# Token norm taken out of the expert stage's input: a raw stream for queries, scores and dot products, and two query units split by token tile

## The chip, the cores and the metric

The kernel runs on 1 core of one Trainium2 chip. The metric is the device time of one execution in microseconds, the median of several. The engines of the core are PE (matmuls, with its weight loads shown apart as PEld), DVE, ACT, POOL and SP; the last two and others issue DMAs.

## The reference

256 tokens of width 1024, float32. A first block (mixing layer, then a product-key expert layer), then a second block of two layers with feed-forward parts. The change touches only the entry of the expert layer:

```python
hn = rmsnorm(h, norm2_g)                       # h * rsqrt(mean(h^2) + eps) * g, per token
qp = (hn @ wq).reshape(128, 8, 2, 128)         # per tile of 128 tokens: 8 heads, 2 halves
s  = einsum('thcd,hcnd->thcn', qp, subkeys)    # 128 scores a half
v1, i1 = top_k(s[:, :, 0], 16); v2, i2 = top_k(s[:, :, 1], 16)
sc, p  = top_k(all 256 sums v1 + v2, 16)       # 16 experts a head, of 16384
gates  = softmax(sc)
act    = gelu(einsum('td,thkd->thk', hn, u[eidx]))
h      = h + einsum('thk,thkd->td', gates * act, v[eidx])
```

## The kernel before

One program with an instruction list per engine; the order of the work is written out by hand and the engines meet at semaphores. The stream is kept as `hT`, features on partitions, 8 blocks of 128 features (`KT`) by 256 tokens; the two tiles of 128 tokens are `own(0)` and `own(1)`. Weights come as "units" of 1 MB through a ring of 4 slots, loaded by SP: 14 for the input projection, 4 for the output projection, 8 query units (`peerq`, one head each), then those of the second block. A unit's weights may be loaded when the unit four before is done (`unit_done`).

Around the change, in order of time:

- Output projection, four units. For each, DVE adds the result to `hT` (L1168, `h_new`) and ACT squares it (L540, `norm_sq`). DVE fills its gaps with `ada_ops`, weighted sums for the second block's modulation.
- Norm: PE sums the squares with a ones matrix (`sums`, L1629), ACT makes Ln and Exp (`rsqrt`, L545 and L547, `norm_rs`), DVE writes `xn = h * norm2 * rstd` in 16 pieces, token tile 0 first (L1172).
- Queries: unit 0 is taken by token tile (`query_first`, L1889); its scores for tile 0 (`scores(0)`, L1865) come between the tiles. Units 1 to 7 run over all 256 tokens (`features`, L1666), with scores of other heads between them. ACT copies queries (L574, L659, L664) and scores (L654) out of PSUM. `BATCH` lists nine batches of scores: batches 0 and 1 are heads 0 and 1 of tile 0, each later one has two heads.
- Behind units 0 to 3 PE transposes `xn` into token rows in PSUM (`row_transposes`, L1852, `hn_t` counts four); DVE multiplies gathered rows with them.
- Selection on DVE (`top_rows`, `top_pairs`, `top_index`, L1180 to L1248) makes indices, `idx_ready`. DVE does batches 0 and 1, waits for `hn_t` 4, and then takes the 256 rows of the u table (128 experts a token, for 2 tiles) one by one (`u_row`, L1271), with the next batch's selection at rows 6, 9, 12 and 15 of every 32.
- POOL issues the gathers (L496), one for each expert slot, 128 rows of 4 KB. `SEQ` is their order: 38 u gathers, then u and v in turn. `GRING` = 16 slots hold them; from the 17th gather on, POOL waits, for each pair, for the uses of the pair 16 before (`u_used`, `v_used`). It waits for the indices of batch 2 at gather 32 (counted from 0).
- PE, after the last scores, sums the ada products column by column (`columns`, L1877, one-column matmuls), and then accumulates the v rows with a diagonal of weights as the stationary operand (`v_row`, L1928). The weights are gate times Gelu of the dot product; ACT makes Gelu (L690) and the diagonals (L698). The last two of the nine batches of scores are in PSUM banks that the v sums of tile 1 take later.
- The first load of subkeys and iota is issued by POOL when all of `hT` is new (L478 to L480, `peer_in`).

Of the kernel before, what the change touches and what calls it, by code (L numbers as in the profile page):

```python
# [19 lines left out]
ALU = mybir.AluOpType  # L20
# [4 lines left out]
D = 1024  # L25
T = 256
KT = D // P
# [71 lines left out]
def build(nc, xT, cols_d, w_d, alibi_d, masks_d, ident_d, tri_d, blk_d, sbmask_d, iota_d, subk_d, rg_d,  # L99
          u_d, v_d, out):  # L100
    with ExitStack() as ctx:
# [267 lines left out]

        gg, gf2 = small[:, 48:56], small[:, 56:64]  # L370
# [77 lines left out]
        def _(pool):  # L448
# [29 lines left out]
            pool.wait_ge(h_new, H_MIX)  # L478
# [48 lines left out]
        def _(act):  # L527
# [120 lines left out]
            rsqrt(1)  # L648

            def scores_in(b):  # L650

                tt, h, n = BATCH[b]
                act.wait_ge(sc_ps, b + 1)
                a.activation(flat(S[f"s{tt}"][:, 2 * h:2 * h + 2 * n, :]), bank[4 + b % 2][:, 0:256 * n], ACT.Copy  # L654
                             ).then_inc(sc_in, 1)
            for j in range(8):
                if j == 0:
                    act.wait_ge(sc_first, 1)
                    a.activation(S["qpT"][:, 0:2, own(0)], bank[5][:, 0:256].rearrange("p (b t) -> p b t", b=2), ACT.Copy  # L659
                                 ).then_inc(q0_in, 1)  # L660
                    scores_in(0)
                    g = UNIT0["peerq"]
                    act.wait_ge(unit_done, g + 1)
                    a.activation(S["qpT"][:, 0:2, own(1)], bank[g % 2][:, 0:256].rearrange("p (b t) -> p b t", b=2),  # L664
                                 ACT.Copy).then_inc(unit_out[g % 2], 1)
                    continue
                read_unit(UNIT0["peerq"] + j, ACT.Copy, flat(S["qpT"][:, 2 * j:2 * j + 2, :]))
                if j == 1:
                    scores_in(1)
                elif j % 2:  # L670
                    scores_in(2 + j // 2 - 1)
# [15 lines left out]
            def gelu(gp):  # L687
# [3 lines left out]
                             S["act"][:, gp // 4, 32 * (gp % 4):32 * (gp % 4) + 32], ACT.Gelu).then_inc(act_gelu, 1)  # L691
# [236 lines left out]
        def _(dve):  # L928
# [427 lines left out]
            dve.wait_ge(hn_t, 4)  # L1356
            for n in range(ROWS):
                u_row(n)
# [264 lines left out]
        def _(pe):  # L1623
# [11 lines left out]

            def unit_start(g, it=0, regs=False):
# [205 lines left out]
            sums(1, range(0, 4))  # L1842
# [379 lines left out]
```

## Time and profile before

| | us |
|---|---|
| median of 3 runs | 1664.23 |
| lowest, highest | 1662.99, 1664.76 |
| the profiled execution's own time | 1667.39 |
| its span, first to last instruction | 1665.6 |

| engine | busy us | share | instructions |
|---|---|---|---|
| PE | 1408.3 | 85% | 7372 |
| PEld | 1036.3 | 62% | 7372 |
| DVE | 1026.2 | 62% | 1832 |
| ACT | 492.8 | 30% | 827 |
| POOL | 588.1 | 35% | 630 |

The profile shows one execution. A busy share is an average over stages with different limits, so each stage is read by itself. "Idle before" an instruction is followed by what released it, as the profile infers it; "issue" means that the engine waited for nothing that the profile shows. A matmul in float32 appears as two records, each with its weight load; ends of matmuls are modelled and overlap the next start.

### The profile page before, as it was taken

The page shows a single profiled execution, that of the slowest core. Times are in us where ns is not written, and L with a number is a line of the kernel's source. Part 1 is how long each engine was busy: PE and PEld are TensorE (multiplying, and loading weights), DVE is VectorE, ACT ScalarE, POOL GpSimd, SP SyncE. Part 2 cuts the span into 40 slices and gives each one's busy share as a digit, 9 for nine tenths or more (in the row PEclk, how much of TensorE's full clock was granted, in tenths as well). Part 3 has the DMA queues.
Part 4 walks back from the last instruction along what each step waited for, and adds up shares of the span by engine and source line. Part 5 has one row for each costly group of instructions (what it writes and reads, how often), then busy time and mean ns, then how long its engine had stood idle before and what let it go on. Part 6 is the DMA issues. An engine that isn't in the chain of part 4 may idle for free.

```text
span 1665.6 us, 20006 instructions
## 1 busy us (share of the span) xinstructions
PE 1408.3 (85%) x7372; PEld 1036.3 (62%) x7372; DVE 1026.2 (62%) x1832; ACT 492.8 (30%) x827; POOL 588.1 (35%) x630
## 2 busy tenths in 40 slices
PE   6889989677777777787777789889999998989998
PEld 5778878322222222332222259889999996789998
DVE  4796669856547464674644455778787447554544
ACT  2222202111111211121121126344444556444342
POOL 1320045566666666666666620012221002100000
PEclk9999998799999998799999999999999998999999
DMA  9655687999999999999899974659885441135450
GB/s 371 254 204 185 252 349 267 366 371 340 380 377 350 353 363 360 365 370 373 336 353 365 371 309 160 245 216 317 315 318 196 139 152 76 68 139 178 184 189 25
DMA packets 113930, 454.10 MB, mean 273 GB/s; under 512 B 12032, under 2 KB 29584, under 8 KB 100544
## 3 DMA queue, kind: packets, MB, share of 16 engines
q0 software_dynamic: 81616, 297.84, 47.4%
q1 hardware_dynamic: 32240, 155.31, 25.6%
q8 instruction: 41, 0.67, 0.2%
q14 instruction: 33, 0.27, 0.0%
HBM read 452.06 MB, written 1.05 MB: 272 GB/s over the span
## 4 chain that ended last, share of the span: by engine, by line
PE 55%; POOL 12%; issue 11%; DMA 10%; DVE 8%; ACT 2%; another core or an unknown queue 1%; SPq 0%; POOLq 0%; DVEq 0%; ACTq 0%
PE psum L2020 14%; POOL arena L496 12%; PE psum L2034 7%; PE psum L1683 7%; PE psum L1928 7%; DMA arena<-v_d,arena 6%; PE psum L1666 6%; DMA arena<-u_d,arena 2%; PE psum L1653 2%; PE psum L1696 1%; PE psum L1877 1%; DVE arena L1271 1%; DVE wlo L955 1%; PE psum L1650 1%
## 5 line engine op out<-in xcount | busy, mean ns | idle before, releaser
L1928 PE MATMUL psum<-arena 128*128 128x512 f32 x952 | 493.4, 651 | 173.2 <-DMA arena<-v_d,arena 125.0
L1928 PEld LDWEIGHTS psum<-arena 128*128 128x128 f32 x952 | 175.0, 201 | 489.4 <-DMA arena<-v_d,arena 277.6
L1271 DVE CUSTOM_DVE_ANT_0 arena<-arena,psum 128x1024 f32<-128x1024 f32 x256 | 305.1, 1219 | 212.7 <-DMA arena<-u_d,arena 167.1
L496 POOL DMA_INDIRECT arena<-u_d,arena x256 | 244.3, 954 | 201.1 <-issue 74.1
L496 POOL DMA_INDIRECT arena<-v_d,arena x256 | 243.3, 950 | 86.4 <-issue 73.2
L955 DVE TENSOR_TENSOR wlo<-ring,whi 128x2048 fp32r<-128x2048 f32 x74 | 169.5, 2291 | 107.8 <-ACT whi L564 107.8
L698 ACT ACTIVATE arena<-ident,arena 128x128 f32<-128x128 f32 x238 | 84.4, 394 | 431.2 <-PE psum L1928 191.1
L2020 PE MATMUL psum<-xh,whi 128*128 128x256 f32 x704 | 201.1, 286 | 9.4 <-DVE xl L949 5.6
L2020 PE MATMUL psum<-xl,whi 128*128 128x256 f32 x704 | 200.5, 285 | 0.0
L2020 PE MATMUL psum<-xh,wlo 128*128 128x256 f32 x704 | 200.4, 285 | 0.0
L564 ACT ACTIVATE whi<-ring 128x2048 fp32r<-128x2048 f32 x74 | 140.7, 1901 | 27.8 <-PE psum L1683 23.4
L2020 PEld LDWEIGHTS psum<-xh,whi 128*128 128x128 f32 x704 | 136.5, 194 | 10.7 <-issue 6.3
L2020 PEld LDWEIGHTS psum<-xl,whi 128*128 128x128 f32 x704 | 136.5, 194 | 0.0
L2020 PEld LDWEIGHTS psum<-xh,wlo 128*128 128x128 f32 x704 | 136.5, 194 | 0.0
L511 POOL DMA_DIRECT2D second<-w_ada x64 | 46.3, 724 | 194.2 <-DVE second L983 113.6
L2034 PE MATMUL psum<-fh,dhi 128*128 128x256 f32 x352 | 100.7, 286 | 0.0
L2034 PE MATMUL psum<-fl,dhi 128*128 128x256 f32 x352 | 100.5, 286 | 0.0
L2034 PE MATMUL psum<-fh,dlo 128*128 128x256 f32 x352 | 100.5, 285 | 0.0
L961 DVE TENSOR_TENSOR dlo<-ring,dhi 128x1024 fp32r<-128x1024 f32 x44 | 53.9, 1225 | 69.0 <-ACT dhi L570 69.0
L570 ACT ACTIVATE dhi<-ring 128x1024 fp32r<-128x1024 f32 x44 | 46.5, 1057 | 137.3 <-PE psum L2034 137.3
L1683 PE MATMUL psum<-xh,whi 128*128 128x256 f32 x288 | 85.0, 295 | 1.8 <-DVE xl L949 1.5
L1683 PE MATMUL psum<-xh,wlo 128*128 128x256 f32 x288 | 82.1, 285 | 0.0
(287 smaller groups left out, 2272.2 us busy)
## 6 DMA issues: line engine op xcount, KB each, us to landing
ring<-w_ffn SPq DMA_DIRECT2D x44, 1536.0 KB, 6.6
second<-w_ada POOLq DMA_DIRECT2D x64, 384.0 KB, 6.5
arena<-w_ada SPq DMA_DIRECT2D x50, 384.0 KB, 7.3
ring<-w_inproj SPq DMA_DIRECT2D x14, 1024.0 KB, 7.9
ring<-w_qkv SPq DMA_DIRECT2D x12, 1024.0 KB, 5.1
ring<-w_l0in SPq DMA_DIRECT2D x10, 1024.0 KB, 4.9
ring<-w_peerq SPq DMA_DIRECT2D x8, 1024.0 KB, 7.7
sq<-w_ada SPq DMA_DIRECT2D x14, 384.0 KB, 6.6
```

The source lines that it names most:

```text
L496: g.indirect_dma_start(S["rows"][:, p % GRING, :], None, u_d if kind == "u" else v_d, bass.IndirectOffsetOnAxis(S["idx"][:, n // SLOTS, n ...
L564: a.activation(r32(S[f"whi{g % 2}"]), slot(g, 0, 2048), ACT.Copy).then_inc(w_hi, 1)
L570: a.activation(r32(S[f"dhi{j % 2}"]), slot(g, 2048, 3072), ACT.Copy).then_inc(d_hi, 1)
L698: a.activation(S["diag"][:, c % DIAGS, :], ident[:, :], ACT.Copy, scale=S["wts"][:, n // SLOTS, n % SLOTS:n % SLOTS + 1]).then_inc(diag_re ...
L955: v.tensor_tensor(r32(S[f"wlo{g % 2}"]), slot(g, 0, 2048), S[f"whi{g % 2}"], ALU.subtract).then_inc(w_lo, 1)
L961: v.tensor_tensor(r32(S[f"dlo{j % 2}"]), slot(g, 2048, 3072), S[f"dhi{j % 2}"], ALU.subtract).then_inc(d_lo, 1)
L1271: v.tensor_tensor_reduce(row, row, xrow[n // SLOTS], 1.0, 0.0, ALU.mult, ALU.add, S["act"][:, n // SLOTS, n % SLOTS:n % SLOTS + 1]).then_i ...
L1666: ins = t.matmul(bank[g % 2][:, b * T:(b + 1) * T], w[:, b, k, :], src[:, k, :], start=(k == 0), stop=(k == KT - 1))
L1683: ins = t.matmul(bank[g % 2][:, b * T:(b + 1) * T], r32(w[i][:, b, k, :]), r32((hi, lo)[j][:, k, :]), start=(b == 0 and k == 0 and i + j = ...
L1928: ins = t.matmul(vacc[tt][:, at], S["diag"][:, c % DIAGS, :], row[:, at], start=(n % SLOTS == 0), stop=(n == LAST_PE[tt]))
L2020: ins = t.matmul(bank[g % 2][:, b * T:(b + 1) * T], r32(w[i][:, b, k, :]), r32((xh, xl)[jj][:, k, :]), start=(b == 0 and k == 0 and i + jj ...
L2034: ins = t.matmul(bank[2 + n // 2][:, 256 * (n % 2):256 * (n % 2) + 256], r32(w[i][:, n, :]), r32(S[f"{('fh', 'fl')[jj]}{u % 2}"]), start=( ...
```

## The change

The token factor of the norm, 1/rms, is the same for all features of a token, so it can be applied behind a matmul. `xn` becomes `h * norm2`, without the factor, written per unit right after each residual add (two instructions of 128x256 instead of four of 128x128). The factor is computed per token on partitions (`token_sums`, one-column matmuls with the squares as stationary operand; `token_rstd` on ACT, 128x2) and applied where the scores leave PSUM (`scores_in`, scale operand) and inside Gelu. The first half of the token sums stands before the last output unit, the second half behind the first query tile.

Query units 0 and 1 are both taken by token tile, tile 0 first: PE's order is query(0, tile 0), second half of the token sums, scores(0), query(1, tile 0), query(0, tile 1), scores(1), two groups of transposes, query(1, tile 1), then units 2 to 7 as before. The transposes of tile 0 thus stand ahead of unit 2, and those of tile 1 behind units 2 and 3. DVE waits for `hn_t` 2 before the first u row and for 4 before row 128. POOL loads subkeys and iota after the recurrent part's transposes (`rec_t` 2).

```diff
@@ POOL
-            pool.wait_ge(h_new, H_MIX)
+            pool.wait_ge(rec_t, 2)
             g.dma_start(S["subk"], subk_d).then_inc(peer_in, 16)
@@ ACT
-            rsqrt(1)
+            def query_in(j, tt):
+                g = UNIT0["peerq"] + j
+                src, dst = (bank[5], bank[1])[j] if tt == 0 else bank[g % 2], S["qpT"][:, 2 * j:2 * j + 2, own(tt)]
+                if tt == 0:
+                    act.wait_ge(sc_first, j + 1)
+                    done = q0_in
+                else:
+                    act.wait_ge(unit_done, g + 1)
+                    done = unit_out[g % 2]
+                a.activation(dst, src[:, 0:256].rearrange("p (b t) -> p b t", b=2), ACT.Copy).then_inc(done, 1)
+            def token_rstd():
+                act.wait_ge(norm_sum, 2)
+                seq.mark(a.activation(lnv[:, 0:2], NORM[:, 0:2], ACT.Ln, scale=1.0 / D, bias=col("eps")))
+                seq.wait()
+                a.activation(rs_tok, lnv[:, 0:2], ACT.Exp, scale=-0.5).then_inc(norm_rs, 1)
             def scores_in(b):
...
+                a.activation(flat(S[f"s{tt}"][:, 2 * h:2 * h + 2 * n, :]), bank[4 + b % 2][:, 0:256 * n], ACT.Copy,
+                             scale=rs_tok[:, tt:tt + 1]).then_inc(sc_in, 1)
+            query_in(0, 0)
+            token_rstd()
+            act.wait_ge(norm_rs, 2)
+            scores_in(0)
+            query_in(1, 0)
+            query_in(0, 1)
+            scores_in(1)
+            query_in(1, 1)
@@ gelu
-                             S["act"][:, gp // 4, 32 * (gp % 4):32 * (gp % 4) + 32], ACT.Gelu).then_inc(act_gelu, 1)
+                             S["act"][:, gp // 4, 32 * (gp % 4):32 * (gp % 4) + 32], ACT.Gelu,
+                             scale=rs_tok[:, gp // 4:gp // 4 + 1]).then_inc(act_gelu, 1)
@@ DVE
-            dve.wait_ge(norm_rs, 2)
-            for tt in range(TT):
-                for k in range(KT):
-                    v.scalar_tensor_tensor(xn[:, k, own(tt)], hT[:, k, own(tt)], col("norm2", k), rstd[:, own(tt)],
-                                           ALU.mult, ALU.mult).then_inc((xg_ready, norm_out)[tt], 1)
+                dve.wait_ge(h_new, j + 1)
+                for k in (2 * j, 2 * j + 1):
+                    v.tensor_scalar(xn[:, k, :], hT[:, k, :], col("norm2", k), None, ALU.mult).then_inc(norm_out, 1)
...
-            dve.wait_ge(hn_t, 4)
+            dve.wait_ge(hn_t, 2)
             for n in range(ROWS):
+                if n == SLOTS:
+                    dve.wait_ge(hn_t, 4)
@@ PE
+            def token_sums(ks):
+                for k in ks:
+                    pe.wait_ge(norm_sq, 8 + k + 1)
+                    for tt in range(TT):
+                        ins = t.matmul(NORM[:, tt:tt + 1], sq[:, k, own(tt)], ones[:, 0:1],
+                                       start=(k == 0 and tt == 0), stop=(k == KT - 1), skip_group_check=True)
...
-            sums(1, range(0, 4))
+            token_sums(range(0, 4))
...
-            sums(1, range(4, KT))
...
+            query(0, 0)
+            token_sums(range(4, KT))
+            scores(0)
+            query(1, 0)
+            query(0, 1)
+            scores(1)
+            row_transposes(0)
+            row_transposes(1)
+            query(1, 1)
+            for j in range(2, 8):
                 g = UNIT0["peerq"] + j
                 unit_start(g)
-                if j == 0:
...
+                features(g, xn)
                 if j < 4:
                     row_transposes(j)
-                if j == 1:
-                    scores(1)
-                elif j and j % 2:
+                if j % 2:
                     scores(2 + j // 2 - 1)
```

`query(j, tt)` is the old `query_first` for both units: for each feature block both column halves in turn, unit 0 tile 0 waiting for each block of `xn`.

## Rows read from the trace of the kernel before

**Rows 1.** The page's chart in 40 slices, the DMA row.
```profile
DMA  9655687999999999999899974659885441135450
```

**Rows 2.** All gathers of the v table by their source line: durations, first and last start.
```profile
L496 POOL DMA_INDIRECT arena<-v_d,arena x256: 932/937/1937, 285.1 to 971.8; - x128
```

**Rows 3.** Stretches: length, busy (count) PE, PEld, DVE, ACT, POOL, clock, DMA share, GB/s.
```profile
220.00:240.00 20.00, 15.10 (x64) 11.88 (x63) 7.78 (x27) 1.19 (x2) 11.22 (x12) 0.86 1.02 411
240.00:260.00 20.00, 19.31 (x93) 16.83 (x92) 19.72 (x60) 2.39 (x4) 10.42 (x12) 0.97 0.96 366
260.00:280.00 20.00, 19.31 (x121) 17.64 (x119) 19.52 (x47) 7.32 (x12) 7.69 (x8) 0.97 0.59 185
280.00:300.00 20.00, 10.69 (x52) 11.15 (x51) 19.90 (x39) 4.23 (x12) 14.99 (x16) 0.50 1.00 381
300.00:320.00 20.00, 12.95 (x34) 7.76 (x35) 14.10 (x53) 1.61 (x4) 7.49 (x8) 0.68 0.87 332
```

**Rows 4.** Timeline of DVE: start, us, line, operation, count, idle before and releaser.
```profile
195.53 0.69 DVE L1168 TENSOR_TENSOR hT<-psum,hT 128x512 f32<-128x512 f32 x1 [4.77 <-PE psum L1666]
198.84 4.29 DVE L1172 SCALAR_TENSOR_TENSOR xn<-hT,cols,rstd 128x128 f32<-128x128 f32 x16 [2.62 <-ACT rstd L547]
...
205.10 0.48 DVE L1180 MAX8 arena<-arena 128x8 f32<-128x128 f32 x2
...
217.32 0.49 DVE L1180 MAX8 arena<-arena 128x8 f32<-128x128 f32 x2 [2.63 <-ACT arena L654]
...
238.82 1.22 DVE L1271 CUSTOM_DVE_ANT_0 arena<-arena,psum 128x1024 f32<-128x1024 f32 x1 [11.70 <-PE psum L1852]
...
246.82 0.48 DVE L1180 MAX8 arena<-arena 128x8 f32<-128x128 f32 x2
...
273.07 0.18 DVE L1245 CAST arena<-arena 128x32 int32<-128x32 f32 x1
```

**Rows 5.** Timeline of PE matmuls, same columns.
```profile
199.34 4.02 PE L1889 MATMUL psum<-xn,ring 128*128 128x128 f32 x32 [1.49 <-DVE xn L1172]
203.84 0.71 PE L1865 MATMUL psum<-arena 128*128 128x128 f32 x4 [0.47 <-ACT arena L659]
204.38 3.74 PE L1889 MATMUL psum<-xn,ring 128*128 128x128 f32 x32
...
238.62 2.07 PE L1865 MATMUL psum<-arena 128*128 128x128 f32 x8
...
275.98 10.26 PE L1877 MATMUL psum<-ones,ring 128*128 128x1 f32 x60
...
309.88 24.15 PE L1928 MATMUL psum<-arena 128*128 128x512 f32 x52
```

**Rows 6.** Timeline of POOL's issues, same columns.
```profile
214.89 1.03 POOL L496 DMA_INDIRECT arena<-u_d,arena  x1 [17.24 <-DVE arena L1245]
...
241.97 0.94 POOL L496 DMA_INDIRECT arena<-u_d,arena  x1 [7.39 <-DVE arena L1271]
...
276.40 0.93 POOL L496 DMA_INDIRECT arena<-u_d,arena  x1 [5.67 <-DVE arena L1271]
...
302.49 0.94 POOL L496 DMA_INDIRECT arena<-v_d,arena  x1 [0.30 <-issue]
314.11 0.94 POOL L496 DMA_INDIRECT arena<-u_d,arena  x1 [10.68 <-PE psum L1928]
```

**Rows 7.** Timeline of PE weight loads around its two slow stretches.
```profile
223.94 5.70 PEld L1666 LDWEIGHTS psum<-xn,ring 128*128 128x128 f32 x27
231.96 0.19 PEld L1666 LDWEIGHTS psum<-xn,ring 128*128 128x128 f32 x1 [2.33 <-issue]
...
291.32 0.29 PEld L1877 LDWEIGHTS psum<-ones,arena 128*128 128x128 f32 x1 [1.33 <-issue]
...
307.51 2.42 PEld L1877 LDWEIGHTS psum<-ones,arena 128*128 128x128 f32 x11 [1.81 <-issue]
```

**Rows 8.** DVE groups by line, first 60 us: count, busy, mean.
```profile
L1009 DVE TENSOR_SCALAR arena<-hT,cols 128x256 f32<-128x256 f32 x8 | 2.2, 346 | 0.0
```

More of the change, by code:

```diff
@@ L367, in flat @@
             return ap.rearrange("p a b -> p (a b)")
+        rs_tok = small[:, 1:3]
         gg, gf2 = small[:, 48:56], small[:, 56:64]
@@ L653, in scores_in @@
                 act.wait_ge(sc_ps, b + 1)
-                a.activation(flat(S[f"s{tt}"][:, 2 * h:2 * h + 2 * n, :]), bank[4 + b % 2][:, 0:256 * n], ACT.Copy
-                             ).then_inc(sc_in, 1)
-            for j in range(8):
-                if j == 0:
[L658 to L666, printed above, removed]
+                a.activation(flat(S[f"s{tt}"][:, 2 * h:2 * h + 2 * n, :]), bank[4 + b % 2][:, 0:256 * n], ACT.Copy,
[9 more added lines that the diff above has]
+            for j in range(2, 8):
                 read_unit(UNIT0["peerq"] + j, ACT.Copy, flat(S["qpT"][:, 2 * j:2 * j + 2, :]))
-                if j == 1:
-                    scores_in(1)
-                elif j % 2:
+                if j % 2:
                     scores_in(2 + j // 2 - 1)
@@ L1857, in scores @@
                 tt, h, n = BATCH[b]
-                if b:
+                if b < 2:
+                    pe.wait_ge(q0_in, b + 1)
+                else:
                     wait_unit_out(pe, UNIT0["peerq"] + h + n - 1)
@@ L1878, in columns, with query @@
                     ins.then_inc(mcol_ps, 1)
-            def query_first(tt):
-                g = UNIT0["peerq"]
+            def query(j, tt):
+                g = UNIT0["peerq"] + j
                 w = slot(g, 0, 2048).rearrange("p (b k c) -> p b k c", b=2, k=KT)
-                at = (bank[5], bank[g % 2])[tt]
-                for b in range(2):
-                    for k in range(KT):
-                        if b == 0:
-                            pe.wait_ge((xg_ready, norm_out)[tt], (KT + 2, KT)[tt] + k + 1)
+                at = (bank[5], bank[1])[j] if tt == 0 else bank[g % 2]
+                if tt == 0:
+                    unit_start(g)
+                elif j == 1:
+                    pe.wait_ge(q0_in, 2)
+                for k in range(KT):
+                    if j == 0 and tt == 0:
+                        pe.wait_ge(norm_out, KT + k + 1)
+                    for b in range(2):
                         ins = t.matmul(at[:, b * P:(b + 1) * P], w[:, b, k, :], xn[:, k, own(tt)],
-                                       start=(k == 0), stop=(k == KT - 1))
+                                       start=(k == 0 and b == 0), stop=(k == KT - 1), skip_group_check=True)
                 ins.then_inc((sc_first, unit_done)[tt], 1)
-            for j in range(8):
+            query(0, 0)
[7 more added lines that the diff above has]
+            query(1, 1)
+            for j in range(2, 8):
                 g = UNIT0["peerq"] + j
                 unit_start(g)
-                if j == 0:
-                    query_first(0)
-                    pe.wait_ge(q0_in, 1)
-                    scores(0)
-                    query_first(1)
-                else:
-                    features(g, xn)
+                features(g, xn)
                 if j < 4:
                     row_transposes(j)
-                if j == 1:
-                    scores(1)
-                elif j and j % 2:
+                if j % 2:
                     scores(2 + j // 2 - 1)
```

4 lines of the change are left out of this document (added).

## The prediction

> **What bounds the kernel now.** I read the page's chart first. DMA stands at 9 tenths from the sixth slice to the twenty-third [rows 1]; a slice is 41.6 us. That is the expert stage: 512 gathers of 128 table rows (0.52 MB each), issued by POOL through a ring of 16 slots, the first at 214.89 us [rows 6], the last at 971.8 [rows 2]. So 757 us of the 1665.6 go by the transfers, one gather every 1.48 us, where POOL alone could issue one in 1.24 (22 issues from 276.40 to 302.49 [rows 6], 26.1/21). PE, DVE and ACT have room in this stage. The stage gets shorter in two ways only: it starts earlier, or the DMA idles less.
>
> Next I looked for that idle time in stretches [rows 3]. From 220 to 240 the share is 1.02, then 0.96, 0.59, 1.00, 0.87. Lost are 0.8 + 8.2 + 2.6 = 11.6 us. The 8.2 comes because POOL may not issue gather 32 before DVE has made the indices of batch 2 (273.07 [rows 4], gather at 276.40 [rows 6]); the 2.6 because the 55th gather needs the slot of the first v row, which PE uses at 309.88 [rows 5], and is let go at 314.11 after 10.68 us [rows 6]. I call that issue the gate. At the gate every slot but one is landed or used, before and after the change alike, so I carry the rest over whole: the end moves as the gate moves, unless the DMA has no idle left to lose.
>
> Why is DVE late? Its first dot product runs at 238.82 after 11.70 us of waiting for the fourth group of transposes [rows 4], which PE reaches only after four query units. And PE is slow there: 27 weight loads follow each other at 0.21 us until 229.6, the next ones are at 231.96 and on with up to 2.33 us of "issue" between, to 237.6 [rows 7]; the same from 290.0 to 307.2 in the column sums [rows 7]. Both begin 14 to 15 us after POOL began a run of issues without a pause (214.89, 276.40) and end 3 to 4 us after it stopped (234.58 and 303.43, from the idle in [rows 6]). The trace shows no cause beyond "issue". I take this as a pattern of two cases, not as a law; the answer hangs on it.
>
> **The change, part by part.**
> *Stream and norm.* Before: last residual 195.53, then sum of squares, Ln and Exp, DVE's 16 multiplies from 198.84 (4.29 us), the first query tile on PE at 199.34, top-16 at 205.10 [rows 4, 5]. Now xn is h times a column: 8 instructions at 0.27 (2.2/8 [rows 8]), six of them in gaps; the last two end at 196.2 + 0.6 = 196.8. Query tile 0 has six of eight k-steps ready when PE leaves the out projection at 195.5. Token sums replace column sums: 16 records per half. They are nowhere in the trace; nearest are the one-column matmuls of the ada sums, 0.22 each at half clock (11 in 2.42 [rows 7]), and for full clock the queries' 0.114 (3.65/32 [rows 5]). So 1.8 to 3.5 us a half; I take 1.8, since the clock stayed full at this place in the queries. First half: 1.8 against 1.9 for the old form, nothing. PE then: query(0,0) 195.7 to 199.4, sums to 201.2, scores(0) 0.5. From scores to top-16 took 205.10 - 203.84 = 1.26 [rows 4, 5]; here Ln and Exp (about 0.95, as from sums to 198.84 before) end at 202.2 and the copy follows, so top-16 starts at 202.8. Gain 2.3 (0.5 to 2.5). The scale operands in the copies and in Gelu cost nothing I can find; the subkey load (1 MB), now at 170 instead of 196.5, is moved past no other POOL work of use and meets an idle-enough DMA.
> *Two units by token tile.* PE: query(1,0), query(0,1), 3.65 each, scores(1) from 209.0: its scores are out at 210.2, before DVE is free at 212.4. Batch 1 starts then instead of at 217.32 [rows 4]: 4.9 us, of which 2.3 were already counted. DVE is through at 222.2.
> *hn_t 2 instead of 4.* Transposes 0 and 1 are done at 210.7. DVE starts its dot products at 222.2 instead of 238.82: 16.6 us. It then needs seven rows and scores(2). Before, that was at 246.82 [rows 4] and scores(2) were out at 240.7 [rows 5]; the wait had a cover of 6 us. Now row 6 lands near 231 (gathers at 1.28 us from 215, two query weights between them) and scores(2), unhindered, are out at 230.3 + 0.8. The cover is gone: whatever PE loses before scores(2) is lost to DVE and to batch 2.
> *PE to the gate.* From the end of scores(2) to the column sums are 35.3 us (240.7 to 276.0 [rows 5]), all weights loaded ahead. Then 48 columns in 96 records: 0.11 each for some 3 us, then 0.22, as the first 60 in 10.26 say [rows 5]; the granted clock there is 0.50 [rows 3]. Then the first v row, 4.2 us to the gate.
>
> **The forecast: both slow stretches come again, as long as before.** The first falls on PE at 227 (14.5 us after 212.6), in query unit 3, and adds 8.0: scores(2) at 238.3 instead of 240.7. DVE's batch 2 starts at 239.1 instead of 246.82, its indices are made at 265.5, gather 32 goes at 268.6. Columns start at 273.6; the second stretch begins at 282.2, after 27 + 25 records. POOL fills its ring by 268.6 + 27 = 295.9, the stretch ends at 300, some 8 records later; 36 are left, 8 us. First v row at 308, gate at 312: 2 us earlier. Of the 16.6 us only 2 arrive, since PE, not DVE, opens the gate. On the profiled execution: 1667.39 (span 1665.6) - 2 = 1665.4; on the median of the runs shown, 3.2 lower, **1662.2**. A gain or loss of 2 comes with the first stretch being 3 us longer or shorter: own range 1660 to 1666.
>
> **Rivals.**
> *No slow stretches on the path.* They could be tied to what PE happened to fetch there. Then scores(2) are out at 231, indices at 258, gather 32 at 262, column sums 265.7 to 284, v row done at 288, before POOL is through with the 54th issue (289). The DMA has work without a gap: 11.6 + 2.3, less 1 for the thin backlog at 262, is 13: 1651. If only the second stretch comes, v row at 300 and gate at 304: 10 us, 1654. For it: 240 to 258 shows PE dense beside gathers and no such stretch. Against it: both were there in the one trace.
> The Trainium skill, page "Runtime: NRT & Kernel Launch", section "Instruction fetch mechanics", says that engines fetch ahead in blocks and that crossing a block is mostly hidden. By that rule alone the slow stretches are no lasting property and this rival holds; the "issue" rows of the trace do not agree with it at these two places.
> *A short first stretch.* It begins a few us later, when scores(2) are nearly out, and hits the rest of the units: gate 6 earlier, 1658.
> *The first stretch gets longer (slower).* Before, it ended when POOL stopped at 234.58, because the ring was full and DVE had not begun. Now DVE frees slots, and POOL goes on until DVE is held at its seventh row: 22 gathers, to 239.6. If the stretch ends 3.5 us after that, PE at 1.6 to 2.4 us a record pair still has 12 pairs of its 21 to do at 243: scores(2) at 245.6, 5 us later than before. Batch 2 is where it was (246.4 against 246.82), gather 32 too, but the column sums start at 281, have 53 records done at 289.6, and end at 315: gate 5 later, 1669. It decides from the point where PE's last scores(2) matmul is later than 240.7. For it: both stretches ended with POOL's stop. Against it: two cases only, and PE may be past unit 3 when it begins.
>
> **How the numbers follow.** Forecast 0.38; no or only one stretch 0.27 (1650 to 1656); short first stretch 0.10; longer one 0.25. Less than 0.2% (3.3 us) can't be told from no change. Faster is below 1660.9: 0.27 + 0.10 + 0.06 of the forecast's low side = 0.43. Slower is above 1667.6: 0.25. Within: 0.32. Gains and losses hold both; the range leaves one in ten on either side: 1651 to 1669.5.
>
> **What will show it.** Top-16 at 202.8; batch 1 without idle before it; the first dot product near 222; then an idle of DVE before batch 2 (the forecast: 7 to 9 us, released by scores; none if no stretch comes; 14 if it is longer). Gather 32 near 269, gate near 312. Wrong would be the whole argument if the stretches from the gate on did not repeat, or if the DMA share after it changed.

## The result, and the profile after

The changed kernel takes 1673.71 us (median of 5 runs, 1671.32 to 1678.61) against 1664.76 of the kernel before beside it (5 runs): ratio 1.006, 95% interval 1.0043 to 1.0077. It is slower by about 9 us, clear of noise (the interval is 7 to 13 us); forecast were 1662.2 with a range up to 1669.5. The profiled execution has a span of 1676.8 us, 11.2 more than before. The last gather of the v table starts at 981.7 instead of 971.8 [rows 2], so nearly all of it is lost before that point.

DVE's timeline (columns as in [rows 4]):
```profile
196.95 0.61 DVE L1187 TENSOR_SCALAR xn<-hT,cols 128x256 f32<-128x256 f32 x2
...
202.66 0.49 DVE L1194 MAX8 arena<-arena 128x8 f32<-128x128 f32 x2 [3.05 <-ACT arena L673]
...
212.17 0.48 DVE L1194 MAX8 arena<-arena 128x8 f32<-128x128 f32 x2
...
221.94 1.21 DVE L1285 CUSTOM_DVE_ANT_0 arena<-arena,psum 128x1024 f32<-128x1024 f32 x1
...
247.20 0.49 DVE L1194 MAX8 arena<-arena 128x8 f32<-128x128 f32 x2 [17.18 <-ACT arena L673]
```
The first four rows are what the change was to do: top-16 2.4 us earlier than in [rows 4], batch 1 5.2 earlier, the first dot product 16.9 earlier. The fifth shows where it went: DVE waits 17.18 us for scores(2), and batch 2 starts at 247.20, where it was at 246.82.

POOL's issues, to be read against [rows 6]:
```profile
212.45 1.03 POOL L497 DMA_INDIRECT arena<-u_d,arena  x1 [40.79 <-DVE arena L1259]
...
238.66 0.94 POOL L497 DMA_INDIRECT arena<-u_d,arena  x1 [0.30 <-issue]
251.57 0.94 POOL L497 DMA_INDIRECT arena<-u_d,arena  x1 [11.98 <-DVE arena L1285]
...
276.79 0.94 POOL L497 DMA_INDIRECT arena<-u_d,arena  x1 [5.67 <-DVE arena L1285]
...
302.88 0.94 POOL L497 DMA_INDIRECT arena<-v_d,arena  x1 [0.31 <-issue]
324.63 0.93 POOL L497 DMA_INDIRECT arena<-u_d,arena  x1 [20.82 <-PE psum L1962]
```
The 22nd gather goes at 238.66 without a break, six more than the 16 of before; gather 32 is where it was; the gate, the 55th, is let go at 324.63 instead of 314.11, after 20.82 us instead of 10.68.

PE's timeline:
```profile
196.02 3.73 PE L1922 MATMUL psum<-xn,ring 128*128 128x128 f32 x32
199.59 1.84 PE L1657 MATMUL psum<-ones,sq 128*128 128x1 f32 x16
...
221.21 5.79 PE L1692 MATMUL psum<-xn,ring 128*128 128x256 f32 x26
...
228.04 0.38 PE L1692 MATMUL psum<-xn,ring 128*128 128x256 f32 x1 [1.04 <-issue]
...
243.45 0.59 PE L1879 MATMUL psum<-ident,xn 128*128 128x128 f32 x2 [1.02 <-issue]
244.36 2.08 PE L1894 MATMUL psum<-arena 128*128 128x128 f32 x8 [0.33 <-ACT arena L575]
...
277.83 5.16 PE L1894 MATMUL psum<-arena 128*128 128x128 f32 x40 [0.69 <-ACT arena L575]
285.92 6.42 PE L1906 MATMUL psum<-ones,ring 128*128 128x1 f32 x31 [2.94 <-ACT arena L673]
292.98 0.16 PE L1906 MATMUL psum<-ones,ring 128*128 128x1 f32 x1 [0.64 <-issue]
...
305.58 0.16 PE L1906 MATMUL psum<-ones,ring 128*128 128x1 f32 x1 [2.63 <-issue]
...
320.10 10.28 PE L1962 MATMUL psum<-arena 128*128 128x512 f32 x19
```
PE is slow from 226.6 to 243.5 (by its weight loads), 16.9 us where it was 8, and scores(2) are out at 246.4 instead of 240.7 [rows 5]: 5.7 lost. The columns begin at 285.92 instead of 275.98: another 4.2 lost between. From there to the v row it is 34.2 (33.9 before).

Of those 4.2, 0.9 are on PE itself: its next 64 records take 15.25 us, where they took 14.34, at a granted clock of 0.92 instead of 0.98. Another 0.2 are in the last scores (5.16 against 4.97), and the remaining 3.1 are on ACT. L574 and L575 are its copies of a query unit, L654 and L673 its copies of the scores. First two of its rows before, then four after:
```profile
231.98 0.60 ACT L574 ACTIVATE arena<-psum 128x512 f32<-128x512 f32 x1 [14.69 <-remote]
...
276.18 0.60 ACT L654 ACTIVATE arena<-psum 128x512 f32<-128x512 f32 x1 [0.41 <-PE psum L1865]
```
```profile
228.76 0.60 ACT L575 ACTIVATE arena<-psum 128x512 f32<-128x512 f32 x1 [14.31 <-remote]
...
281.02 0.69 ACT L673 ACTIVATE arena<-psum,small 128x512 f32<-128x512 f32 x1 [0.42 <-PE psum L1894]
285.18 0.69 ACT L673 ACTIVATE arena<-psum,small 128x512 f32<-128x512 f32 x1 [3.47 <-remote]
291.60 0.69 ACT L673 ACTIVATE arena<-psum,small 128x512 f32<-128x512 f32 x1 [5.73 <-remote]
```
ACT has slow stretches of its own, and its first one begins sooner than PE's. Query unit 2 is through on PE at 223.8 before and at 220.9 after; ACT copies it only at 231.98 and 228.76, some 8 us later. Nothing on the path waits for that copy. The second one does cost: the copy at 285.18 is the eighth, for which the columns wait (`sc_in` 8); the one at 291.60 is the ninth, for which they do not. Before, all nine copies were through by 276.8, just as gather 32 was issued (276.40). After, the copies are 6.7 us later and gather 32 is not, and the last two are caught. Whether ACT had such a stretch there before too can't be seen: from 280.0 on it had nothing to do until DVE's 32nd dot product was out (291.6).

The windows (columns as in [rows 3]) sum it up: DMA share 0.83 where it was 0.96, and 0.45 where it was 0.87. That is 2.6 and 8.4 us of transfers lost, 11.0 together; the span grew by 11.2.
```profile
220.00:240.00 20.00, 10.09 (x41) 7.42 (x40) 9.84 (x21) 0.60 (x1) 14.99 (x16) 0.79 1.02 412
240.00:260.00 20.00, 16.96 (x70) 14.33 (x70) 12.53 (x46) 1.88 (x3) 4.68 (x5) 0.78 0.83 320
...
300.00:320.00 20.00, 12.79 (x62) 13.16 (x61) 15.43 (x55) 0.20 (x1) 2.90 (x4) 0.50 0.45 180
```

### The profile page after: what moved, and what is told of

Same layout as the page of the kernel before. It is cut to its first block, busy times and chain, and to the rows that moved or that the text cites. A ratio compares the mean times of both kernels' runs of the same rounds, so it can differ in the third digit from the quotient of the medians.

```text
span 1676.8 us, 20097 instructions
## 1 busy us (share of the span) xinstructions
PE 1414.7 (84%) x7420; PEld 1044.8 (62%) x7420; DVE 1023.5 (61%) x1824; ACT 494.9 (30%) x828; POOL 586.7 (35%) x630
## 4 chain that ended last, share of the span: by engine, by line
PE 52%; POOL 14%; issue 12%; DMA 10%; DVE 7%; another core or an unknown queue 3%; ACT 2%; POOLq 0%; SPq 0%; DVEq 0%
PE psum L2054 14%; POOL arena L497 14%; PE psum L2068 7%; PE psum L1709 7%; DMA arena<-v_d,arena 7%; PE psum L1962 5%; PE psum L1692 4%; PE psum L1679 2%; PE psum L1906 2%; DMA arena<-u_d,arena 2%; PE psum L1722 1%; DVE arena L1285 1%; PE psum L1676 1%; PE psum L1824 1%
## 5 line engine op out<-in xcount | busy, mean ns | idle before, releaser
L2054 PE MATMUL psum<-xl,whi 128*128 128x256 f32 x704 | 200.5, 285 | 0.0
L2054 PE MATMUL psum<-xh,wlo 128*128 128x256 f32 x704 | 200.4, 285 | 0.0
L1709 PE MATMUL psum<-xl,whi 128*128 128x256 f32 x288 | 82.7, 287 | 0.0
```

Source lines behind the costliest of these rows:

```text
L1709: ins = t.matmul(bank[g % 2][:, b * T:(b + 1) * T], r32(w[i][:, b, k, :]), r32((hi, lo)[j][:, k, :]), start=(b == 0 and k == 0 and i + j = ...
L2054: ins = t.matmul(bank[g % 2][:, b * T:(b + 1) * T], r32(w[i][:, b, k, :]), r32((xh, xl)[jj][:, k, :]), start=(b == 0 and k == 0 and i + jj ...
```

## The experiments

They ran on six chips, and there are two kinds. On some the kernel before takes 1664 to 1668 us and the slow stretches are there; on the others it takes 1590, and none is seen in any trace. Each ratio is to the kernel before on the same chip. In the quoted expectations the letters of the theories hold for that text alone; from e12 on, A2 is that POOL's run of issues brings the stretch about, B2 that the busy DMA does.

**Holding the gathers back (e1, e7, e13, e15).** The edit, before POOL's 17th gather:
```diff
+                if p == GRING:
+                    pool.wait_ge(sc_in, 3)
```


> The changed kernel with one wait more: POOL issues gather 16 only when the scores of batch 2 are copied out (sc_in 3), so that its first run of issues ends after 16 gathers, as in the kernel before. Theory A (PE's slow stretch lasts until POOL stops issuing): POOL stops at about 232, PE is fast again at 235 to 236, scores(2) end near 238 instead of 246.4, DVE's idle before batch 2 shrinks from 17.2 to 8 or 9 us, the 55th gather goes near 313 to 316 instead of 324.6, and the time falls from 1673.7 to 1662 to 1666. Theory B (the stretch belongs to what PE fetches there or to a busy DMA, which stays busy for some 20 us after the 16th gather): PE is slow until 243 as before, the scores end at 246, nothing is gained, 1673 to 1676.

> The changed kernel with POOL's gather 16 held until the scores of batch 2 are out. Where the slow stretches occur, theory A (a stretch lasts until POOL stops issuing): scores(2) end near 238, gate 313 to 316, 7 to 11 us faster than the changed kernel. Where there are none, the hold has nothing to shorten: scores(2) are out near 231, the ring is full then anyway for a moment only, and it is within 2 us of the changed kernel.

> The changed kernel with GpSimd held before the 17th gather until scores(2) are out. On a chip with slow stretches: the first one ends 3 to 4 us after the 16th issue, DVE idles 9 to 10 us before batch 2, the 55th gather is released at 315 to 318, and the time is 6 to 9 us below the changed kernel, within 3 us of the kernel before. On a chip without them: 8 to 10 us below the kernel before, as the changed kernel itself.

> The changed kernel with GpSimd held before the 17th gather until scores(2) are out. On a chip with slow stretches: the first one ends 3 to 4 us after the 16th issue, DVE idles 9 to 10 us before batch 2, the 55th gather is released at 315 to 318, and the time is 6 to 9 us below the changed kernel, within 3 us of the kernel before. On a chip without them: 9 to 11 us below the kernel before, as three runs of this edit gave.


The first three met chips without stretches: 1580.61, ratio 0.9941 (0.9925 to 0.9958); 1579.65, 0.9945 (0.9928 to 0.9961); 1580.27, 0.9933 (0.9909 to 0.9957). There the wait costs nothing and gains nothing against the changed kernel unedited:

**The changed kernel on other chips (e6, e8).**


> The changed kernel itself, unedited, beside the kernel before on one and the same chip. In the first experiments the kernel before took 1590 us and not 1664, with a DMA share of 1.02 to 1.03 all through the gathers and no slow stretch of PE. Theory A1 (the change costs time where the slow stretches occur and gains where they do not, as the rival without slow stretches had it): if this chip shows none, DVE's wait before batch 2 is under 3 us, the column sums begin near 266, the 55th gather is not late, and the time is 9 to 13 us below the kernel before. If it shows them, the scores of batch 2 end at 246, the gate is at 320 to 325, and the time is 7 to 11 us above it. Theory B1 (the change costs the same everywhere, by its own order of work): 7 to 11 us above the kernel before in either case.

> The changed kernel once more, for the comparison on this chip. Without slow stretches 8 to 10 us below the kernel before, with them 7 to 11 us above it. Both theories of the extra PE work are read against this run.


e6 (no stretches): 1581.34, ratio 0.9944 (0.9927 to 0.9961), 8 us faster. e8 (stretches): 1677.67 against 1668.48, ratio 1.0046 (1.002 to 1.0071), 9 us slower. So the same edit gains 8 us on one kind of chip and loses 9 on the other, and theory B1 is out. PE of e6:
```profile
225.03 7.07 PE L1692 MATMUL psum<-xn,ring 128*128 128x256 f32 x32
...
232.79 1.16 PE L1894 MATMUL psum<-arena 128*128 128x128 f32 x8 [0.25 <-ACT arena L575]
...
269.11 8.74 PE L1906 MATMUL psum<-ones,ring 128*128 128x1 f32 x60
277.70 7.82 PE L1906 MATMUL psum<-ones,arena 128*128 128x1 f32 x36
285.38 9.71 PE L1962 MATMUL psum<-arena 128*128 128x512 f32 x16
```
No record with "issue" stands in it (its times lie some 4 us later than in the first profile: the first gather is at 216.27). Unit 3 takes 7.07 us, the columns run through, the v row is done before POOL needs its slot, and POOL never waits at the gate.

In e15 the stretches were there: 1669.81 against 1663.76, ratio 1.0045 (1.0023 to 1.0068), where I expected within 3 us of the kernel before. Half of the expectation held: POOL stops at 232.0, PE's last late weight load is at 234.9, scores(2) start at 236.82, DVE idles 9.43 us. But the issues that were held back make a new run, from 240.00 to 254.7, and ACT is late in it: it copies unit 5 at 257.13, though PE was through with it at 252.3, and PE waits 5.45 us for that. DVE is sooner, with more dot products behind it, gather 32 goes at 270.60, and ACT is caught in the score copies for longer:
```profile
257.13 0.60 ACT L577 ACTIVATE arena<-psum 128x512 f32<-128x512 f32 x1 [11.07 <-remote]
...
280.47 0.69 ACT L675 ACTIVATE arena<-psum,small 128x512 f32<-128x512 f32 x1 [3.17 <-remote]
291.70 0.69 ACT L675 ACTIVATE arena<-psum,small 128x512 f32<-128x512 f32 x1 [10.55 <-remote]
```
The columns start at 296.70, and the gate opens at 321.74. Mending the first stretch alone leaves the kernel 6 us above the kernel before. The changed kernel itself did not run on this chip; on the two others of its kind it was 9 above, with intervals that overlap this one. So the stretch got shorter, as theory A has it, but no gain in time is shown.

**Taking parts (e2, e3, e4), on a chip without stretches.** e2 is the changed kernel with DVE's `wait_ge(hn_t, 4)` back; e3 and e4 move the columns of the changed and of the old kernel behind the v rows, one group each (first the edit of e2):
```diff
-            dve.wait_ge(hn_t, 2)
+            dve.wait_ge(hn_t, 4)
```
```diff
-            pe.wait_ge(sc_in, 8)
-            columns(0, 0, 16, MCOL_AT[0])
...
                 v_row(c, n)
+                if c == 0:
+                    pe.wait_ge(sc_in, 8)
+                if c < 16:
+                    columns(0, c, c + 1, MCOL_AT[0] + 3 * c)
```


> The changed kernel with DVE's first dot product waiting for the fourth group of transposes again (hn_t 4), one part undone; everything else of the change stays. Theory A: the ring is full after 16 gathers, POOL stops at 232, PE's slow stretch ends at 236, the fourth group is done near 237, DVE starts there instead of at 221.9 and needs the seven rows (8 us): batch 2 near 246, as in the kernel before; gate 313 to 316, time 1662 to 1667. Theory B: the stretch goes on to 243, DVE starts at 244, batch 2 at 252, 5 us later than in the changed kernel, time 1676 to 1680.

> The changed kernel with the 16 groups of column sums moved from before the first v row to behind v rows 0 to 15, one group each. If the gate (the 55th gather, let go by the first v row) is what made the changed kernel slower, it opens as soon as PE is through the scores and the weights are ready: first v row near 295 instead of 320, gate near 299 to 303 instead of 324.6, no idle DMA from 305 to 320; time 20 us lower, 1650 to 1658. If the gate's time is made up for later (the stream bound by the DMA over its whole length), the time stays within 3 us of 1673.7. A second slow stretch during the last scores may hold the first v row at 305 to 310: then 1658 to 1664.

> The kernel before with the same move of the column sums. Gate theory: scores end at 276, first v row when its weights are ready near 295 and not at 310, gate at 299 instead of 314.1, of which the DMA can use only what it idled (2.6 us from 300 to 320 by its share): 1658 to 1662. Beside the changed kernel with the same move it says what the change is worth once the column sums are off the path: by the theory that the early start of DVE is eaten by PE's slow stretch, these two are within 5 us of each other.


e2: 1586.26, ratio 0.9979 (0.9965 to 0.9992). DVE waits 6.73 us for the transposes before its first dot product and gather 32 is at 267.11, 4.1 to 4.5 us later than in e1 and e3 on the same chip (262.65, 262.97). So 5 to 6 of the 9 to 10 us gained there are DVE's earlier start. The other 4 may be the earlier first gather; no run took it alone. e3: 1581.36, 0.9946 (0.9929 to 0.9962); e4: 1590.57, 1.0 (0.9991 to 1.001). Where no stretch falls on them, the columns are not on the path in either kernel.

e4 stands in for the kernel before on such a chip. Its windows 220 to 300 have DMA shares of 0.96, 1.02, 0.80 and 1.00, those of e6 1.02, 1.02, 0.98 and 1.02; that is 5.2 us of transfers. From its first gather to its last it is 669.8 us (219.5 to 889.3), in e6 664.1 (216.3 to 880.4).

**Both edits with stretches (e5), and more work ahead of scores(2) (e10, e11).**


> The changed kernel with POOL's gather 16 held until the scores of batch 2 are out, and with the column sums behind the first 16 v rows. Without slow stretches neither wait nor gate binds: within 2 us of the changed kernel. With them: scores(2) near 238, first v row near 295 to 305, 15 to 20 us below the changed kernel and 5 to 10 below the kernel before.

> The changed kernel with PE made 13.8 us later before the scores of batch 2: the 32 records of query unit 3 are executed three times in all, into the same PSUM bank, with the result of the last. It stands in for the slow stretch on a chip that has none. Chain theory (what PE loses before scores(2), DVE's batch 2, gather 32 and the stream lose): batch 2 starts 12 to 13 us later than in the changed kernel, gather 32 too, the DMA idles for 9 to 12 us between 255 and 285, and the time is 9 to 12 us above the changed kernel (1590 to 1593 where that takes 1581). Rival: the ring and the busy DMA hide it, less than 3 us.

> The kernel before with unit 3's records executed twice, PE 6.9 us later. There DVE waits for all four groups of transposes, so its first dot product moves by 6.9 us. Chain theory: 4 to 7 us above the kernel before. If it is so, the kernel before with 6.9 us of lateness is slower than the changed one with 13.8 by 2 to 7 us, and twice the lateness alone does not make the change slower: the second stretch must have its share too.


e10's edit (e11: `again(g, xn, 1)` in the old kernel), where `again` repeats the unit's matmuls into the same bank ahead of the real ones:
```diff
+                if j == 3:
+                    again(g, xn, 2)
                 features(g, xn)
```
e5 is the wait of e1 and the move of e3 together. All on the chip of e8. First a row of POOL and the last late weight load of PE in e8, then the same of e5:
```profile
254.23 0.93 POOL L497 DMA_INDIRECT arena<-u_d,arena  x1 [12.59 <-DVE arena L1285]
...
245.75 0.18 PEld L1879 LDWEIGHTS psum<-ident,xn 128*128 128x128 f32 x1 [0.43 <-issue]
```
```profile
242.64 0.94 POOL L499 DMA_INDIRECT arena<-u_d,arena  x1 [8.82 <-issue]
...
236.96 0.71 PEld L1694 LDWEIGHTS psum<-xn,ring 128*128 128x128 f32 x2 [0.42 <-issue]
```
e5: 1669.88, ratio 1.0013 (1.0 to 1.0026), 8 us below e8, where I expected 15 to 20, and not below the kernel before, where I expected 5 to 10. POOL stops at 233.8 instead of 241.6 and PE is at pace from 237.0 instead of 245.7: on one and the same chip the stretch ends when the issues end. Batch 2 starts at 241.91, 8 us earlier than in e8, and the columns no longer stand ahead of the first v row; that row is now itself late (304.67, with 5.42 us of "issue"), and the gate opens at 321.70 instead of 326.82. Here too ACT is late in the run that follows (unit 5 copied at 259.90, after 11.17 us). It is the best that undoing both losses gave: the loss is gone, no gain has come. In e10 unit 3's records run three times, 13.8 us of PE work more: 1692.72, ratio 1.0137 (1.0113 to 1.0162), 15 us above e8; the 9 to 12 of the expectation were for a chip without stretches. DVE waits 33.06 us for scores(2), the gate is at 341.62, 14.8 later. In the changed kernel, what PE loses before scores(2) reaches the end in full: there is no cover. In e11 the kernel before does unit 3 twice, 6.9 us more: 1671.91, ratio 1.0034 (1.0016 to 1.0053), 3.4 us. It does not test the cover of some 6 us that the prediction named (scores(2) out at 240.7, needed at 246.8), since the repeated unit delays the transposes as well: DVE's first dot product moves to 247.80, batch 2 to 255.80, and the scores, copied by 249.8, still have their 6 us. Gather 32 and the gate come 8 and 6 us later, counted from the first gather; where the rest of the 6.9 went after the gate no run took apart.

**Breaking the run of issues (e12, e14, e16).** In every trace with stretches so far PE's first one began 13.8 to 14.8 us after POOL's run of issues did (the table below). The edit gives POOL a pause within that time:
```diff
+                if p in (10, 42):
+                    pool.wait_ge(row_in[(p - 2) % GRING], 16 * ((p - 2) // GRING + 1))
```


> GpSimd waits, before it issues the 11th and the 43rd gather, until the gather two places earlier has landed; nothing else is altered. Theory A2, a slow stretch is set off by GpSimd issuing gathers without a break (in six traces with slow stretches it began 13.5 to 14.8 us after the start of the run of issues): on a chip with slow stretches none begins near 227, scores(2) come near 232, the MAX8 of batch 2 near 233 instead of 247 to 250, the columns take 0.22 us a record without a break, the 55th gather's release comes near 295, and the time is 10 to 15 us below the kernel before. Theory B2, the stretch goes with the busy DMA and a short break in issuing does not matter: TensorE is slow from 227 as before and the time is that of the changed kernel or up to 3 us above it. On a chip without slow stretches both expect within 2 us of the changed kernel there, 7 to 10 us below the kernel before.

> GpSimd waits, before it issues the 11th and the 43rd gather, until the gather two places earlier has landed (where it was tried without slow stretches this broke the issuing for 10.6 and 6.5 us and cost 5 to 6 us). Theory A2, a slow stretch is set off by GpSimd issuing gathers without a break: on a chip with slow stretches none begins at 227; scores(2) come near 232, the MAX8 of batch 2 by 237, the columns take 0.22 us a record without a break, and the time is 8 to 15 us below the kernel before. Theory B2, the stretch goes with the busy DMA and a break in issuing does not matter: TensorE is slow from about 227 as before, and the time is that of the changed kernel or up to 8 us above it. On a chip without slow stretches both expect what it gave there before: 2 to 5 us below the kernel before.

> The kernel before with the same two breaks in GpSimd's issuing (before the 11th and the 43rd gather, each until the gather two places earlier has landed). Theory A2: on a chip with slow stretches TensorE keeps its pace from 229 to 238, scores(2) come near 231 instead of 238.6, DVE does not wait for them, and the time is 2 to 10 us below the kernel before. Theory B2: TensorE is slow from about 229 all the same and the time is 0 to 8 us above the kernel before. On a chip without slow stretches both expect 0 to 7 us above.


e12 (no stretches): 1587.41, ratio 0.9978 (0.9968 to 0.9989), 7 us above e13 beside it: the pauses of 10.6 and 6.5 us cost that, where within 2 of the changed kernel was expected. e14 (the same kernel, on the chip of e15): 1659.73, ratio 0.9986 (0.997 to 1.0003), 10 us below e15. e16 (the kernel before, same chip): 1663.79, ratio 0.9996 (0.9973 to 1.0018), where 2 to 10 us of gain were expected. POOL, PE and ACT of e14:
```profile
230.82 0.94 POOL L499 DMA_INDIRECT arena<-u_d,arena  x1 [6.33 <-DMA arena<-u_d,arena]
...
256.44 0.94 POOL L499 DMA_INDIRECT arena<-u_d,arena  x1 [3.52 <-DVE arena L1287]
```
```profile
220.99 7.07 PE L1694 MATMUL psum<-xn,ring 128*128 128x256 f32 x32
227.90 0.60 PE L1881 MATMUL psum<-ident,xn 128*128 128x128 f32 x4
228.75 1.16 PE L1896 MATMUL psum<-arena 128*128 128x128 f32 x8 [0.25 <-ACT arena L577]
229.75 13.98 PE L1694 MATMUL psum<-xn,ring 128*128 128x256 f32 x64
257.74 2.08 PE L1896 MATMUL psum<-arena 128*128 128x128 f32 x8 [14.02 <-issue]
```
```profile
226.46 0.60 ACT L577 ACTIVATE arena<-psum 128x512 f32<-128x512 f32 x1 [12.23 <-remote]
...
257.09 0.60 ACT L577 ACTIVATE arena<-psum 128x512 f32<-128x512 f32 x1 [19.64 <-remote]
```
Unit 3 takes 7.07 us and scores(2) start at 228.75, as without stretches; in e15 beside it PE was slow from 226.7. ACT is late all the same (unit 2, through on PE at 220.7, is copied at 226.46), but nothing waits for it. After the pause the loss comes back on ACT: PE is through with unit 5 at 243.7, at pace, and ACT copies it at 257.09, 4.2 us after the issues stopped. Scores(3) need that copy (257.09 + 0.60 = 257.69, and PE starts at 257.74), so PE's 14.02 us of "issue" are a wait for ACT. Whether PE itself would have been slow there can't be seen; it had no work. e16 shows the same in the kernel before: POOL pauses 5.33 us until 232.77, PE runs at pace from 208 to 247.1, and then ACT's next copy comes at 255.57 after 14.72 us and PE's scores at 256.23. The first stretch of PE in a table (us, by its weight loads: end of the last one at pace, start of the last late one):
```
kernel        run of issues starts   PE slow from   issues stop   PE slow until
before               214.89             229.6          234.6          237.6
changed              212.45             226.6          239.6          243.5
e8                   214.51             228.4          241.6          245.7
e10                  213.98             227.8          241.1          245.1
e5                   214.11             228.0          233.8          237.0
e15                  212.28             226.7          232.0          234.9
e11                  215.69             230.5          235.4          238.4
```
The core of theory A2 holds for PE: in both kernels a pause of 5 to 6 us kept it at pace where it had been slow (for the kernel before, in a trace of another chip). B2, that only the busy DMA counts, does not hold (the DMA share is 1.02 from 220 to 240 in e14 as in the changed kernel). The pause waits for a gather to land, though, so it also empties the queue of gathers that are issued and not landed; whether the length of the run counts or the length of that queue was not tested. The price was wrong: I expected 8 to 15 us of gain and got 4, with an interval that touches none, because in the next run ACT is late where PE needs it.

**More pauses (e17, e18, e19).** e19 pauses before gathers 10, 20, 42 and 52 (counted from 0), by the same two lines with `if p in (10, 20, 42, 52):`; e17 and e18 before every tenth of all 512, until the gather four (e17) or two (e18) places earlier has landed.


> The changed kernel with four breaks, before the 11th, 21st, 43rd and 53rd gather, each until the gather two places earlier has landed. Theory A2: on a chip with slow stretches none is seen on TensorE between 225 and 290, scores(3) and the columns come without a break, and the time is 4 to 12 us below the kernel before. Theory B2: some stretch of 10 us or more lies in this part all the same, and the time is at or above that of the kernel before. On a chip without slow stretches: 3 to 10 us above the changed kernel.

> The changed kernel; before every tenth of the 512 gathers GpSimd waits until the gather four places earlier has landed. Theory A2 (a stretch begins about 13 us after the start of an unbroken run of issues, and any break starts the count again): on a chip with slow stretches hardly a stretch is left, and the time falls to between 1585 and 1625 us, 40 us or more below the kernel before. If a break must be longer than the 3 to 4 us that this one gives (theory A3), the stretches stay and the time is within 10 us of the changed kernel. Theory B2, the stretches go with the busy DMA: as A3. On a chip without slow stretches: 0 to 15 us above the changed kernel, for the pauses in the DMA's supply.

> The same with a wait for the gather two places earlier, so breaks of about 6 us. Theory A2: few or no stretches on a chip that shows them, but each break leaves the DMA about 1 us short of work, 51 times; 1600 to 1660 us. Theory A3: the same as A2 here, below the kernel with the short breaks. Theory B2: stretches stay and the breaks are added, above 1680 us. On a chip without slow stretches: 20 to 60 us above the changed kernel.


All three met a chip without stretches, so they tell only the price: e19 1593.47, ratio 1.0018 (1.0002 to 1.0034), 12 us above what the changed kernel gave on such chips, where 3 to 10 were expected; e17 1646.07, 1.0345 (1.0319 to 1.037), 65 above, where 0 to 15 were expected; e18 1778.4, 1.1182 (1.116 to 1.1205), 197 above, where 20 to 60 were. The breaks themselves sum to 105 and 218 us (POOL's idle that a landing gather ended). Waiting for a landing starves the DMA: I had taken too little for the time from issue to landing.

## Why the prediction was wrong

1. The parts of the change went as worked out: top-16 202.66 (forecast 202.8), batch 1 212.17 (212.4), first dot product 221.94 (222.2), scores(1) starting at 208.97 (209.0), the token sums 1.84 (1.8) at full clock. A term put at nothing was not quite nothing: with a scale operand a score copy takes 0.69 us instead of 0.60 and Gelu 0.32 instead of 0.23.
2. The step that failed is the forecast's "both slow stretches come again, as long as before". The first was 16.9 us long instead of 8, because POOL went on issuing for 22 gathers; held to 16 it was 8.2 and 9.0 long (e15, e5). The gate, forecast at 312, opened at 324.63: 8.1 of the 12.6 us between them are scores(2), forecast out at 238.3 and out at 246.4, 4.2 the way from there to the columns (39.5 instead of 35.3). The text had the right rule as a rival ("The first stretch gets longer"): 22 gathers till 239.6 (measured: 238.66 + 0.94 = 239.6), slow till 243 (243.5), scores(2) at 245.6 (246.4), batch 2 at 246.4 (247.20). That its scores(2) came so near is in part luck: it had 12 pairs of records left at 243, and 10 records were. The rival follows from the same observation on which the forecast rested, that a stretch begins some 14 us after the run of issues (14.7 and 13.6 in the trace, not "14 to 15") and ends 3 to 4 after its stop. Given 22 gathers instead of 16, "as long as before" contradicted it. The chances 0.38 and 0.25 were the wrong way round.
3. That rival too was short, 1669 against 1673.7: it put the gate 5 later, measured 10.5. It carried PE's delay to the columns unchanged (281; measured 285.92). Missing are 0.9 us of PE at a lower clock behind the stretch and 3.1 us of ACT, which the prediction never looked at for slow stretches. The trace of before had a sign of them: ACT's copy of unit 2 at 231.98, some 8 us late. How much of it falls on the path varies: in e8 the columns wait for ACT less (0.79 us in front of them), and the gate still comes 112.3 us after the first gather, as in the first trace (112.2; 99.2 before). That ACT's part reaches the end is read from the traces; no run took it alone.
4. "No slow stretches" (0.27) was no rival on this chip but the case on others. There the change gains 8 to 9 us where the rival had 13: it compared with a kernel before that still had its stretches.
5. The point where it decides was right: DVE's earlier start takes away the cover of 6 us under scores(2). The changed kernel shows it (DVE waits 17.18 us for them, and not at all before), and e10 shows that what is then lost arrives in full. That the kernel before could take 6 us more there for nothing was not run: e11 delays the transposes too.

Open: what a slow stretch is, and why some chips show none. The Trainium skill, page "Runtime: NRT & Kernel Launch", section "Instruction fetch mechanics", says that engines fetch instructions by a DMA of their own and mostly hide it. One guess is a fetch that is held up behind queued gathers. The traces do not bear it out: in the profile of before the DMA queues marked "instruction" start no transfer from 214 to 246 nor from 278 to 314, in the changed kernel none from 232 to 262, and yet PE is back at pace at 237.6, 307.5 and 243.5. (Whether the profile lists every such transfer is not known.) Not settled either: whether many short pauses would pay on a chip with stretches, and what starts ACT's stretches, which come sooner than PE's: some 9 us after the first gather it is late already, and after gather 32 of the changed kernel from 4.9 us on. The short breaks before that (5.67 us and less) may not have ended the run for ACT.

No version was fastest on both kinds of chip. The changed kernel as it is gives 0.9944 on one and 1.0046 to 1.006 on the other; the one with two pauses 0.9978 and 0.9986, the second within noise of no change.

## What to carry to other kernels

An engine that starts earlier also frees buffers earlier, and so lets another engine issue for longer; write down how long each run of issues becomes, and apply what the trace shows of runs to its new length before giving the case a chance. When a part of the path moves by a few us, look for the stalls that lie just beside it on every engine, not only on the one that bounds: what fell on harmless work may now fall on the path. An "issue" need not be such a stall, though: PE's 14.02 us in e14 end 0.05 us after the copy of ACT that PE needs, so see first what each instruction depends on. And a change that moves a kernel by half a per cent in a stage bound by DMA is to be timed on more than one chip.

## What the runs showed of the hardware

- The same program takes 1590 us on some chips and 1664 to 1668 on others. The mean granted clock is lower on the latter (0.976 in e6, 0.948 in e8), but a PE that waits more has a lower one anyway: e18 has 0.926 on a chip where the kernel before has 0.975. During the gathers the chart has 409 GB/s in slice after slice on the former and 336 to 380 on the latter. Within a stretch, though, the DMA is not slower: 411 GB/s from 227 to 244 in the changed kernel, against 409 from 233 to 258 in e6. What is lost is lost afterwards, when POOL waits for late engines: its idle time in the gathers that PE, DVE or "remote" ended is 145 us in the changed kernel and 53 in e6, and the gathers take 769 and 664 us.
- In a slow stretch of the columns PE does single records with gaps of 0.57, 1.24, 1.94 and 2.64 us, steps of 0.70. It happened on PE, ACT, DVE (8.05 us of "remote" before 796.46 in the kernel before) and POOL (5.04 before 539.05), each at its own time. From 220 to 880 the changed kernel has 91 idle times of over 1.5 us that end in "issue" or "remote" on these engines (55 on ACT, 21 on DVE, 12 on PE, 3 on POOL) in the first trace, and none in e6.
- PE's first stretch begins 13.8 to 14.8 us after the start of the first unbroken run of gather issues and ends 3 to 4 us after its stop (the table above). The one in the columns begins less regularly (13.6 us after gather 32 before, 15.7 in the changed kernel, 11.3 in e8) and ends as regularly, 4 us after the stop (2 in e14 and e16). A pause of 5 to 6 us kept PE at pace where it had been slow.
